# Turning the norms' results by halves and mixing the last projection into the differential attention

## What is computed

```python
for i in range(DEPTH_2):
    ...
    x = layer_norm(ALPHA * x + y, ln_mix_g[i], ln_mix_b[i])
    f = conv_ffn(x, ffn_w_gate[i], ffn_w_up[i], ffn_conv_w[i], ffn_conv_b[i], ffn_w_down[i])
    x = layer_norm(ALPHA * x + f, ln_ffn_g[i], ln_ffn_b[i])
    x = x + jax.nn.sigmoid(x @ ple_w_gate[i]) * (p[i] @ ple_w_proj[i])
```

## Time and profile before

| | us |
|---|---|
| median of three runs | 1731.55 |
| the three runs | 1720.55, 1732.02, 1731.55 |
| the profiled execution | 1732.88 |
| its span in the profile | 1731.0 |

### The profile page before, as it was taken

One profiled execution on the slowest core, in us unless ns is written; L12 is line 12 of the kernel. 1 busy time (PEld: TensorE's weight loads), 2 busy tenths in 40 slices (PEclk: granted clock), 3 DMA queues, 4 the chain that ended last, 5 costly groups with the idle time before them and its releaser, 6 DMA issues.

```text
span 1731.0 us, 22940 instructions
## 1 busy us (share of the span) xinstructions
PE 1631.3 (94%) x9736; PEld 1390.6 (80%) x9736; DVE 1085.1 (63%) x1320; ACT 856.8 (49%) x1014; POOL 8.2 (0%) x18
## 2 busy tenths in 40 slices
PE   7999999999998999999989978999998997999998
PEld 3787968899985777889888856799986975899986
DVE  4677563545656788975466556665556666665555
ACT  5554543535435777764344356454434346354433
POOL 0000000000000000000000000000000000000000
PEclk9899999999998999999999989999999999899999
DMA  6635302236545799995544322555553422455540
GB/s 233 240 122 204 121 14 77 74 98 213 205 146 207 285 343 349 366 371 195 167 146 158 101 73 91 178 176 189 170 195 122 157 95 90 170 185 181 171 170 25
DMA packets 132301, 297.49 MB, mean 172 GB/s; under 512 B 5175, under 2 KB 16744, under 8 KB 131240
## 3 DMA queue, kind: packets, MB, share of 16 engines
q1 hardware_dynamic: 130336, 287.94, 48.1%
q0 software_dynamic: 1104, 5.52, 1.0%
q10 hardware_dynamic: 760, 2.58, 0.4%
HBM read 294.97 MB, written 1.05 MB: 171 GB/s over the span
## 4 chain that ended last, share of the span: by engine, by line
PE 80%; DVE 11%; ACT 7%; issue 1%; DMA 1%; ACTq 0%; DVEq 0%
PE bank L444 78%; DVE cut L1449 4%; ACT cut L2426 3%; PE bank L457 1%; ACT arena L2623 1%; DVE stat L1673 1%; ACT pairs L2432 1%; DVE XT L2292 1%; DVE pairs L2299 0%; DVE XT L2286 0%; ACT arena L2632 0%; DMA arena<-in_hy 0%; DMA raw<-in_w_in 0%; DVE pairs L1457 0%; DVE stat L2272 0%
## 5 line engine op out<-in xcount | busy, mean ns | idle before, releaser
L1449 DVE TENSOR_TENSOR cut<-raw,cut 128x2048 fp32r<-128x2048 f32 (+1 forms) x266 | 601.3, 2275 | 378.3 <-ACT cut L2426 377.6
L444 PE MATMUL bank<-pairs,cut 128*128 128x256 f32 (+1 forms) x5480 | 690.3, 287 | 20.7 <-DVE cut L1449 8.8
L444 PEld LDWEIGHTS bank<-pairs,cut 128*128 128x128 f32 (+1 forms) x5480 | 677.3, 192 | 33.3 <-issue 15.7
L2426 ACT ACTIVATE cut<-raw 128x2048 fp32r<-128x2048 f32 (+1 forms) x266 | 502.2, 1899 | 308.0 <-PE bank L444 296.1
L444 PE MATMUL bank<-cut,pairs 128*128 128x512 f32 (+1 forms) x2460 | 587.9, 398 | 14.5 <-DVE cut L1449 10.3
L444 PEld LDWEIGHTS bank<-cut,pairs 128*128 128x128 f32 x2460 | 460.7, 191 | 128.8 <-DVE cut L1449 12.6
L444 PE MATMUL bank<-arena 128*128 128x128 f32 (+10 forms) x748 | 177.6, 394 | 17.2 <-ACT arena L2459 6.1
L444 PEld LDWEIGHTS bank<-arena 128*128 128x128 f32 (+4 forms) x748 | 107.6, 190 | 66.9 <-issue 45.4
L2432 ACT ACTIVATE pairs<-arena 128x256 fp32r<-128x256 f32 (+1 forms) x81 | 37.4, 496 | 79.9 <-DVE arena L2336 51.5
L1457 DVE TENSOR_TENSOR pairs<-arena,pairs 128x256 fp32r<-128x256 f32 (+1 forms) x81 | 40.1, 527 | 32.5 <-ACT pairs L2432 32.4
L457 PEld LDWEIGHTS bank<-cst,arena 128*128 128x128 f32 x264 | 31.9, 147 | 30.8 <-issue 12.6
(11 more groups left out here) (294 smaller groups left out, 891.5 us busy)
## 6 DMA issues: line engine op xcount, KB each, us to landing
raw<-in_moe_w_gate SPq DMA_DIRECT2D x32, 1024.0 KB, 7.0
raw<-in_moe_w_up SPq DMA_DIRECT2D x32, 1024.0 KB, 6.7
raw<-in_moe_w_down SPq DMA_DIRECT2D x32, 1024.0 KB, 6.1
raw<-in_w_in SPq DMA_DIRECT2D x30, 1024.0 KB, 5.2
raw<-in_w_mod SPq DMA_DIRECT2D x24, 1024.0 KB, 5.2
raw<-in_ffn_w_gate SPq DMA_DIRECT2D x22, 1024.0 KB, 5.1
raw<-in_ffn_w_up SPq DMA_DIRECT2D x22, 1024.0 KB, 5.1
raw<-in_ffn_w_down SPq DMA_DIRECT2D x22, 1024.0 KB, 5.0
```

The costliest lines, as they stand in the source:

```text
L444: return pe.matmul(o, l, r, start=start, stop=stop, skip_group_check=True)
L1449: v.tensor_tensor(both[:, PIECE:PIECE + n], M.raw[K.place(i)[0]][:, 0:n], both[:, 0:n].bitcast(F32), ALU.subtract).then_inc(*up("lo_w", i))
L2426: a.activation(M.cut[K.slot(i)][:, 0:n], M.raw[K.place(i)[0]][:, 0:n], ACT.Copy).then_inc(*up("hi_w", i))
```

## The change

Four edits:

- Turn by halves. After the first norm three halves are transposed before the ffn, the fourth after the ffn's first 24 matmuls, and VectorE subtracts (0,0) and (1,0) first. After the second norm block 0 is transposed before `pp`; `pg` takes its first two pieces together, uses both for block 0, then block 1 is transposed (`turns`), and then both are used for block 1.
- The turn before the differential layer is split: four feature tiles before the last block of `pg` (`turn_features`), four after the first 24 matmuls of the projection.
- The differential layer's last projection is called in parts: two pieces between the last steps, the other two at the end. Norm roots of pairs 0 and 1 are taken together in step 7, with a second buffer for the spread.
- Cuts are placed by hand at the new positions; some waits drop their level.

```diff
...
-        self.RQc, self.RRc = t1[2], t1[3]
+        self.RQc, self.RRc = t1[2], [t1[3], f(b + 9728, 512)]
...
-    def rows(key, w, X, nk, r0, tile, ready, first, last_, free, among, order, place=None, label=None, hook=None):
+    def rows(key, w, X, nk, r0, tile, ready, first, last_, free, among, order, place=None, label=None, hook=None,
+             turns=None):
...
-                P.wait_ge(*at(*ready(k0 + k)))
+                P.wait_ge(*at(*(ready(k0 + k, i) if turns else ready(k0 + k))))
...
         tail = max(0, nk - 4) if last_ else nk
-        for k0 in range(0, tail, 2):
+        if turns:
+            pieces = [(take(w, r0 + k0, 2, 0, 1024), k0) for k0 in (0, 2)]
+            for i in range(2):
+                for q in range(2):
+                    for h, k0 in pieces:
+                        last = tiles(h, k0, i, q)
+                        if i and q:
+                            leave(h, last)
+                if i == 0:
+                    turns()
+        for k0 in range(4 if turns else 0, tail, 2):
...
-    def mix_out(i, X):
-        rows(("mx", i), D[("ab_w_out", "c_w_out")[i]], X, 8, 0, lambda k: k, X.ready, True, True,
-             lambda b, q: ("z", ("ln", i, 0), b, q), Q, BLOCKS)
...
-    def turn_tokens(key, name):
-        ahead[0] = 1
...
-                for t in range(4):
...
+    def mix_out(i, X, k0=0, n=8, banks=Q):
+        rows(("mx", i), D[("ab_w_out", "c_w_out")[i]], X, n, k0, lambda k: k0 + k, lambda k: X.ready(k0 + k), k0 == 0,
+             k0 + n == 8, lambda b, q: ("z", ("ln", i, 0), b, q), banks, BLOCKS, None, ("mxp", i, k0))
+    def turn_tokens(key, name, halves, pieces):
+        ahead[0] = pieces
+        for b, j in halves:
+            o = claim(("tr", key, b, j), ("lo", name, b, j), (2 * b + j,))
+            P.wait_ge(*at("xn", key, b, j))
+            for t in range(4):
+                m = 4 * j + t
+                last = turned(o[:, 128 * t:128 * t + 128], M.XT[:, b, m * 128:m * 128 + 128])
+            last.then_inc(*up("tr", key, b, j))
         ahead[0] = AHEAD
-    def ffn(i, X):
+    def turn_features(key, src, name, js, banks):
+        before, ahead[0] = ahead[0], 0
+        for j, b_ in zip(js, banks):
+            o = claim(("tr", key, j), ("lo", name, j), (b_,))
...
+                P.wait_ge(*at("xn", key, b, j // 2))
+                for t in range(2):
...
+                    last = turned(o[:, x:x + 128], src[:, b, m * 128:m * 128 + 128])
+            last.then_inc(*up("tr", key, j))
+        ahead[0] = before
...
+    def ffn(i, X, turns):
...
+                        if (c, x, k0, q) == (0, 0, 0, 0):
+                            turns()
...
     def after_mixer(i, X):
-        mix_out(i, mixed[i])
-        turn_tokens(("ln", i, 0), f"XSl{i}")
...
+        turn_tokens(("ln", i, 0), f"XSl{i}", ((0, 0), (0, 1), (1, 0)), 1)
+        K.mark["ffn", i] = taken[0]
+        ffn(i, Op(X.hi, X.lo, lambda k: ("lo", f"XSl{i}", 1, k // 4)),
+            lambda: turn_tokens(("ln", i, 0), f"XSl{i}", ((1, 1),), 0))
+        K.mark["ple", i] = taken[0]
+        turn_tokens(("ln", i, 1), f"XSf{i}", ((0, 0), (0, 1)), 1)
         ple_project(i)
-        turn_tokens(("ln", i, 1), f"XSf{i}")
-        rows(("pg", i), D["ple_w_gate"][i], X, 8, 0, lambda k: k, lambda k: ("lo", f"XSf{i}", 1, k // 4), True, True,
-             lambda b, q: ("pga", i, b, q), A4, HALVES)
+        rows(("pg", i), D["ple_w_gate"][i], X, 8, 0, lambda k: k, lambda k, b: ("lo", f"XSf{i}", b, k // 4), True, True,
+             lambda b, q: ("pga", i, b, q), A4, HALVES, None, None,
+             (lambda: turn_features("x3", M.XT, "XC2", (0, 1), (4, 6))) if i == 0 else None,
+             lambda: turn_tokens(("ln", i, 1), f"XSf{i}", ((1, 0), (1, 1)), 0))
...
+    mix_out(0, mixed[0])
     after_mixer(0, M.XS)
-    turn_block("x3", M.XT, parts=2, name="XC2")
...
-        group(name, m0, W, c0, 4, (X,), 8, lambda m: ("rn", name, m), hook=lambda: hooks.pop(0)())
+        if n:
+            group(name, m0, W, c0, 4, (X,), 8, lambda m: ("rn", name, m), hook=lambda: hooks.pop(0)())
+        else:
+            K.mark["x3"] = taken[0]
+            steps = [lambda: turn_features("x3", M.XT, "XC2", (2, 3), (5, 7))] + 3 * [lambda: None]
+            group(name, m0, W, c0, 4, (X,), 8, lambda m: ("rn", name, m), banks=(0, 2), each=lambda: steps.pop(0)())
...
         if i >= 5 and i % 2 == 1:
-            norm_sums(("c", (i - 5) // 2), M.RQc, 4, (1,))
-        if i >= 5 and i % 2 == 0:
-            norm_spread(("c", (i - 6) // 2), M.RRc, 512)
+            norm_sums(("c", (i - 5) // 2), M.RQc, 4, (((i - 5) % 4) + 1,))
+        for j in {8: (0, 1), 10: (2,), 12: (3,)}.get(i, ()):
+            norm_spread(("c", j), M.RRc[j % 2], 512)
...
-    for i in range(5):
+    banks = (2, 4, 5, 7)
+    for i in range(3):
         differential_step()
-    ahead[0] = AHEAD
+    mix_out(1, mixed[1], 0, 2, banks)
     differential_step()
+    mix_out(1, mixed[1], 2, 2, banks)
+    differential_step()
+    differential_step()
+    mix_out(1, mixed[1], 4, 4, banks)
     after_mixer(1, M.XS)
...
-    def turned_parts(key, name, dst):
-        for j in range(4):
+    def turned_parts(key, name, dst, js=range(4)):
...
             src = M.bank[K.bank("tr", key, j)][:, :].rearrange("p (j t) -> p j t", j=2)
-            w(*at("hi", name, j))
+            w(*at("hi", name, j)[:2])
...
-            w(*at("hi", dst, b, j))
+            w(*at("hi", dst, b, j)[:2])
...
         sums(1, 1)
+        if which:
+            second(0, 0)
+            second(0, 1)
+            cut_until(K.from_mark(("ple", i), 2))
         deviation(1)
         gain(1, 0)
         root(1)
         offset(1, 0)
-        gain(1, 1)
-        offset(1, 1)
-        for b in range(2):
-            for j in range(2):
-                second(b, j)
+        if which:
+            cut_until(K.from_mark(("ple", i), 3))
+            gain(1, 1)
+            offset(1, 1)
+            second(1, 0)
+        else:
+            gain(1, 1)
+            second(0, 0)
+            second(1, 0)
+            offset(1, 1)
+            second(0, 1)
+            cut_until(K.from_mark(("ffn", i), 2))
+        second(1, 1)
...
+                if i == 0 and q and b == 0:
+                    turned_parts("x3", "XC2", M.XC2, (0, 1))
...
-    turned_parts("x3", "XC2", M.XC2)
+    cut_until(K.from_mark("x3", 2))
+    turned_parts("x3", "XC2", M.XC2, (2, 3))
...
-        if i in (1, 3, 6, 8):
-            cut_until(K.from_mark("cv", {1: 3, 3: 4, 6: 5, 8: 6}[i]))
-        if i >= 5 and i % 2 == 1:
-            norm_spread(("c", (i - 5) // 2), roots[0], M.RRc)
-        if i >= 5 and i % 2 == 0:
-            j = (i - 6) // 2
+        pairs = {8: (0, 1), 10: (2,), 12: (3,)}.get(i, ())
+        for j in pairs:
+            norm_spread(("c", j), roots[j % 2], M.RRc[j % 2])
+        for j in pairs:
             x = M.MX[:, 2 * j:2 * j + 2, :]
             normed(("c", j), x.rearrange("p a t -> p (a t)"), SLN)
             cut_lo("XSm1", j, M.XS.lo[:, 2 * j:2 * j + 2, :], x, M.XS.hi[:, 2 * j:2 * j + 2, :])
+        if i in (1, 3, 6, 9, 11):
+            cut_until(K.from_mark("cv", {1: 3, 3: 4, 6: 5, 9: 6, 11: 7}[i]))
...
         first(0, 0)
-        root(1)
-        first(0, 1)
-        first(1, 0)
+        if which:
+            first(0, 1)
+            cut_until(K.from_mark(("ple", i), 2))
+            root(1)
+            cut_until(K.from_mark(("ple", i), 3))
+            first(1, 0)
+        else:
+            root(1)
+            first(0, 1)
+            first(1, 0)
+            cut_until(K.from_mark(("ffn", i), 2))
         first(1, 1)
...
+                if i == 0 and q and b == 0:
+                    turned_parts("x3", "XC2", M.XC2, (0, 1))
...
-    turned_parts("x3", "XC2", M.XC2)
+    cut_until(K.from_mark("x3", 2))
+    turned_parts("x3", "XC2", M.XC2, (2, 3))
...
-        if i in (0, 2, 5, 7):
-            cut_until(K.from_mark("cv", {0: 3, 2: 4, 5: 5, 7: 6}[i]))
...
-        if i >= 5 and i % 2 == 1:
-            norm_root(("c", (i - 5) // 2), roots[0], 1e-5)
-        if i >= 5 and i % 2 == 0:
-            j = (i - 6) // 2
+        for j in {7: (0, 1), 9: (2,), 11: (3,)}.get(i, ()):
+            norm_root(("c", j), roots[j % 2], 1e-5)
+        for j in {8: (0, 1), 10: (2,), 12: (3,)}.get(i, ()):
             w(*at("nn", ("c", j)))
             cut_hi("XSm1", j, M.XS.hi[:, 2 * j:2 * j + 2, :], M.MX[:, 2 * j:2 * j + 2, :])
+        if i in (0, 2, 5, 8, 10):
+            cut_until(K.from_mark("cv", {0: 3, 2: 4, 5: 5, 8: 6, 10: 7}[i]))
...
```

## The result

The changed kernel took 1733.16 us (median of 20 runs, 1730.05 to 1738.60) and the kernel before, run beside it, 1723.35 us (20 runs, 1720.06 to 1732.02): a ratio of 1.0052 with a 95% interval of 1.0040 to 1.0064, or +9.0 us. (The medians themselves lie 9.8 apart.) The forecast was 1734 and "within 1%", and both hold. But the forecast started from the 1731.55 of three runs and added 2.4; the change itself is nearly four times that size. That the time came out within 1 us was luck: the start was too high by 8 and the sum too low by about 7. The size of the change is what the rest is about.

The account below looks back on a forecast made before the run. TensorE, busy for 94% of the span, was taken to bound the kernel, through its stops and clock level. Terms -3.6 +10.8 -5.0 +0.2 = +2.4 us on the 1731.55 median gave 1734, range 1722 to 1744.

Parts of the forecast that it names:

- The first wait of a gate: Before the gate's first matmul: TensorE waits for piece 1 from 1309.0 until 1313.1, 1.1 us earlier than before.
- the one before piece 3: Middle of the gate: piece 3 must wait for piece 0's held slot, so TensorE stands for 3.0 us.
- The turn of block 1: Inside the gate, after block 0's matmuls: eight transposes, then their copy and subtraction come back, +1.9 us.
- The first gate as a whole: Second norm and gate, first layer: -1.1+1.9+3.0+1.65 is +5.4 us; +10.8 for both places, bounds +4 and +14.
- Rival (1): Whole change works as meant, pieces ready whenever TensorE comes to them: some -27.5 us, 1704; chance 0.07.
- Rival (2): Only the mixer works, its fourth piece cut in time, while the gates stall: -4.9 us, 1727; chance 0.2.
- Rival (3): Half clock lasts 10.1 us, not 3.3, in all five holes of gates and mixer: +17 us, 1751; chance 0.05.
- Rival (4): Whole kernel: the change does nothing that shows, since holes only move: 1731; chance 0.1.
- First norms: Two places: ffn starts 1.3 us earlier, half a clock stretch saved (-0.8 each); sum -3.6 us, bounds -0.5 and -5.3.
- The mixer: Last projection: begins 10.1 us earlier, but TensorE stands from 1470.1 to 1475.7; sum +0.2 us, bounds -3 and +4.
- The second layer's gate: Second norm and gate, second layer: same waits and one 1.65 us clock cost as in the first, +5.4 us.
- The split turn: Before the differential layer's projections: hole and half clock go, 2.0 us of transposes return; -5.0 us, bounds -3 and -5.5.

Follow-up runs that it names:

- the mended kernels: Changed kernel with both mends (gate: one piece held, block 1's aggregate and half-turn earlier; mixer: fourth piece cut within steps), run twice: 1703.43 and 1703.77 us.
- gate only: The kernel before with only the second norms' and gate's part of the change: ratio 1.0079 to the kernel before, +13.6 us.
- split turn only: The kernel before with only the split turn before the differential layer: ratio 0.9966 to the kernel before, -5.9 us.
- mixer only: The kernel before with only the mixer's last projection begun between the last steps: ratio 1.0019 to the kernel before, +3.3 us.
- the kernel with earlier cuts: Changed kernel, two gate pieces still held, with two cuts and block 1's root moved ahead on ScalarE and VectorE: ratio 0.9998 to the kernel before.
- the kernel with one piece held: Changed kernel holding only the first gate piece between token blocks, the second taken after block 1's turn: ratio 0.9926 to the kernel before, -12.8 us.

## Why the prediction was right, and where its sizes were off

Right were the sign of each term and nearly every wait. The first wait of a gate was forecast at 4.1 us (1309.0 to 1313.1) and was 3.82; the one before piece 3 at 3.0 and was 3.08; the mixer's at 5.6 and was 5.67. The turn of block 1 was forecast at +1.9 and took 2.02 (1315.42 to 1317.44). The first gate as a whole was forecast at +5.4 and came at +5.7. The experiments show the causes that the forecast named: with one piece fewer in the slots the waits of the gate go but one, with cuts ahead of the copies the first one shrinks, with the fourth piece cut in the steps the mixer's goes. Rival (1), that it works as meant (1704), fell by the three waits; the mended kernels came to that time, 1703.4, once these were gone, though here too by the start that was 8 too high: as a change they are -21 to -23, not -27.5. Rival (2) fell by the 5.67. Rival (3) holds in one of its five places: the stretch at 0.50 reached 10.2 us only around the mixer's tail, where half of it lay over the hole; behind the gates' holes it was 3.4, 3.4, 3.4 and 6.8. Rival (4), nothing that shows, is excluded by the interval of the ratio; with 20 runs each, 0.5% could be told from no change, where the prediction put the limit at about 1%.

The sum was +2.4 and the trace's difference +7.9. Three terms make up 5.8; the first gate's +0.3 and the split turn's -0.6 bring it to the 5.5:

- **First norms, -3.6 forecast, -1.7 in the trace, -1.6 alone.** The ffn was to start 1.3 us earlier; it started 1.1 earlier at the first place (29.85 to 28.74 since the projection's start) and 0.7 at the second. The transposes inside the ffn cost 0.36 each (1107.45 to 1107.81), not 0.5. (The 24 matmuls ahead of them were priced at 5 us; by the row that is named, 4.82 for 21, it is 5.5, and 5.41 was measured. Nothing hung on it.) The further 0.4 from a piece cut sooner didn't come. And "I take half" of a clock stretch held at one place only: at the first, TensorE's work at 0.50 after the ffn's start was 5.0 us before (from 1107.5) and lasted from 1102.20 to 1107.5 after, no less; at the second it ended 6.0 us after the ffn's start before (1495.6 to 1501.6) and 4.1 after (1492.4 to 1496.5), which is 0.9 us of time. Even this isn't shown to come from the edit. From the end of the mixer's projection to the ffn's tail at i = 1 the kernel before took 189.5 us and the changed one 188.4, but the three kernels that leave the first norms as they were (gate only, split turn only, mixer only) took 188.3, 188.2 and 188.5: only the trace of before has a stretch of 10.2 us at 0.50 there, theirs have 6.8. So what is left of the term is the -0.6 of the first place.
- **The mixer, +0.2 forecast, +2.15 in the trace.** Its first piece was forecast 10.1 us earlier; within the stage it is 9.0 earlier. The steps ahead of it ran at 0.50 from 1441.5 to 1449: the four broadcasts at 1444.01 took 3.75 us; the two at 1459.02 in the kernel before took 1.10 at full clock. The prediction had put that stretch under the first piece and charged half of one, 0.8; it was two, ahead of it. The other 0.9 stands between the second piece and the hole: the two broadcasts at 1465.65 took 1.88 instead of 1.1, and the spread's wait 1.39 was walked through as 1.2.
- **The second layer's gate, +5.4 forecast, +7.35 in the trace.** Its waits are the first layer's to the hundredth (3.82, 0.98, 3.08). Its second stretch at 0.50 was 6.8 us with 5.98 of work in it, where the first layer's was 3.4 with 3.10: that is 1.4 of the 1.95, and the first gate's surplus of 0.3 is in this one too. The forecast had priced every hole by the shortest stretch seen and given the longer ones only to rival (3), all or none. A price of 1.65 to 3.4 for each hole, as a bound of the main sum, would have been nearer.

The split turn was forecast at -5.0 and gave -5.6 in the trace, -5.9 alone; its inputs came in time, as walked.

One more size was off, not in the prediction but in an expectation: what the second held piece costs. It was given 4 us a gate, a wait traded for a wait. Taking it away gave 10.9 a gate by the ratios (9.6 by the traces), because the wait that took its place was short and had no half clock behind it, and because a product that asks for one piece at a time also waits for less at its start.

## What to carry to other kernels

With n slots, count how many are held by pieces that stay over a second use: each is a slot that the next cuts don't have, and with three slots and two held the next piece starts only when the first is left. Take pieces one at a time, reuse only the one that covers the late operand (block 1's turn), and put cuts in each queue ahead of whatever waits for another engine (here a root behind an aggregate behind a cut). Parts of a joined change can be timed alone; here that showed at once that one of four lost 13.6, while two others gained 5.9 and perhaps 1.6.

## What the runs showed of the hardware

- The clock at 0.50 comes in stretches of 3.4, 6.8 and 10.2 us, once 13.7 (1458 to 1472, the kernel with earlier cuts), and the same instructions with the same waits can get different ones: behind the 3.08 us wait of the gate it was 3.4 us in the first layer and 6.8 in the second, within one execution. The same wait can also get none: the one of 2.09 us before the ffn's tail (2.08 in some) stands at both layers in all 14 traces, and a stretch of 3.4 followed it in 20 of the 28 places; in the kernel with both mends it did at the first layer (48 matmuls in 13.02 us) and not at the second (11.47). The waits of 3.08 and 3.82 were followed by one each time, one of 1.98 in either gate of the kernel with one piece held was not, nor were those of 1.07 and 0.98. What decides stays open, so a difference of 1.5 us between two traces can be the clock alone.
- Stretches at 0.50 that lie over holes cost nothing, so the clock's cost, as an estimate, is half of TensorE's busy time within them, not half of their length: some 3 us here and not 6.8. Where TensorE was busy throughout, a stretch of 3.4 cost 1.50 (24 matmuls, 7.38 against 5.88) and 1.55 (48, 13.02 against 11.47).
- Switching ScalarE's table took 1.28 us in the changed kernel too, and the next activation began 0.01 us later (1440.78 + 1.28 = 1442.06, next at 1442.07).
- The kernel before spread over 12 us in 20 runs (1720.06 to 1732.02), more than the change. A median of three was 8 us off, and the 14 profiled executions came to the first mixer's projection, up to which no edit reaches, at 1069.1 to 1077.7.
